# Loads and layer norm around the mixing stage of an encoder layer: weights moved behind the last output product, first tile's norm spread over four tiles, first tile reordered

## The reference

```python
proj = x @ w_in                                   # 1024 -> 2048: gate b, gate c, value, pool input (512 each)
y_conv = gate_b * short_conv3(gate_c * value)     # depthwise, centred, 3 taps
y_pool = (window_mean(pool_in, 2/4/8/16) - pool_in) @ pool_w * pool_scale   # per group of 128 channels
x1 = layer_norm(alpha * x + concat(y_conv, y_pool) @ w_out, g1, b1)
y = layer_norm(alpha * x1 + square(relu(x1 @ w_ff1)) @ w_ff2, g2, b2)
```

## Time and profile before

| | |
|---|---|
| median of 6 runs | 1308.21 us (1306.96 to 1308.37) |
| profiled execution, time | 1307.83 us |
| profiled execution, span of its slowest core (core 5) | 1306.3 us |
| spans of the eight cores | 1296.3 to 1306.3 us |
| TensorE busy in that span | 94% |
| VectorE, ScalarE, GpSimd busy | 48%, 18%, 11% |

### The profile page before, as it was taken

One profiled execution on the slowest core, in us unless ns is written; L12 is line 12 of the kernel. 1 busy time (PEld: TensorE's weight loads), 2 busy tenths in 40 slices (PEclk: granted clock), 3 DMA queues, 4 the chain that ended last, 5 costly groups with the idle time before them and its releaser, 6 DMA issues.

```text
span 1306.3 us, 16633 instructions; the slowest of 8 cores (1296.3 to 1306.3 us)
## 1 busy us (share of the span) xinstructions
PE 1233.2 (94%) x5760; PEld 565.1 (43%) x5760; DVE 620.7 (48%) x948; ACT 239.9 (18%) x497; POOL 140.6 (11%) x158
## 2 busy tenths in 40 slices
PE   4899979999955999999999999999999999999996
PEld 3544434444422444444444444444444444444442
DVE  1457446444501813853581482376348148435324
ACT  2322112222200310320230031023013003202300
POOL 4335234321400000000000000000000000000000
PEclk9999998999987999999999999999999999999998
DMA  9963775975599442361242245226124423702001
GB/s 135 187 127 84 172 145 170 219 148 177 128 197 241 142 130 97 107 184 65 97 144 83 97 137 154 97 89 187 31 110 136 127 97 113 178 33 98 1 1 65
DMA packets 75106, 160.90 MB, mean 123 GB/s; under 512 B 38544, under 2 KB 38544, under 8 KB 71824
## 3 DMA queue, kind: packets, MB, share of 16 engines
q1 hardware_dynamic: 63984, 119.59, 27.4%
q0 software_dynamic: 11040, 40.24, 19.2%
HBM read 126.66 MB, written 56.62 MB: 140 GB/s over the span
## 4 chain that ended last, share of the span: by engine, by line
PE 87%; DMA 9%; DVE 1%; issue 1%; POOL 1%; ACT 0%; DVEq 0%; ACTq 0%; SPq 0%; POOLq 0%
PE bank L281 87%; DMA ring<-xe 6%; DMA scr_xb<-ring 1%; DMA scr_z<-ring 1%; DMA win<-w_in 1%; DVE ring L288 1%; POOL H L292 0%; DVE H L292 0%; DVE H L288 0%; ACT H L285 0%; PE bank L358 0%; ACT L285 0%; ACT win L285 0%; DVE st L462 0%; DVE wff L288 0%
## 5 line engine op out<-in xcount | busy, mean ns | idle before, releaser
L281 PE MATMUL bank<-xT,wff 128*128 128x512 bf16 x2048 | 447.7, 381 | 30.8 <-DVE ring L288 30.8
L281 PEld LDWEIGHTS bank<-xT,wff 128*128 128x128 bf16 x2048 | 201.1, 98 | 276.2 <-issue 37.6
L288 DVE SCALAR_TENSOR_TENSOR ring<-ring,bank 128x512 f32<-128x512 f32 x128 | 81.5, 684 | 462.2 <-PE bank L281 381.7
L285 ACT ACTIVATE H<-bank 128x512 f32<-128x512 f32 (+1 forms) x292 | 169.2, 591 | 368.3 <-PE bank L281 267.0
L281 PE MATMUL bank<-win,H 128*128 128x512 bf16 x1024 | 224.1, 379 | 0.0
L292 DVE TENSOR_TENSOR H<-H 128x512 bf16<-128x512 f32 x256 | 173.2, 687 | 82.4 <-ACT H L285 82.1
L281 PE MATMUL bank<-wout,H 128*128 128x512 bf16 x768 | 171.4, 382 | 4.4 <-DVE wff L292 4.4
L281 PEld LDWEIGHTS bank<-win,H 128*128 128x128 bf16 x1024 | 100.2, 98 | 120.8
L281 PE MATMUL bank<-xT,win 128*128 128x512 bf16 (+1 forms) x608 | 118.8, 356 | 24.7 <-DMA win<-w_in 16.7
L292 POOL TENSOR_TENSOR H<-H 128x527 f32<-128x527 f32 (+2 forms) x80 | 100.8, 1260 | 226.0 <-ACT H L285 188.0
L281 PEld LDWEIGHTS bank<-wout,H 128*128 128x128 bf16 x768 | 75.6, 98 | 96.5 <-issue 7.1
(11 more groups left out here) (35 smaller groups left out, 347.5 us busy)
## 6 DMA issues: line engine op xcount, KB each, us to landing
ring<-xe SPq DMA_DIRECT2D x32, 512.0 KB, 15.4
scr_x<-ring SPq DMA_DIRECT2D x32, 512.0 KB, 2.8
ring<-scr_x SPq DMA_DIRECT2D x32, 512.0 KB, 9.7
y<-ring SPq DMA_DIRECT2D x32, 512.0 KB, 2.9
scr_z<-ring SPq DMA_DIRECT2D x28, 512.0 KB, 14.0
ring<-scr_z SPq DMA_DIRECT2D x28, 512.0 KB, 5.7
wff<-w_ff POOLq DMA_DIRECT2D x8, 1024.0 KB, 19.9
scr_xb<-ring POOLq DMA_DIRECT2D x32, 256.0 KB, 4.0
```

What stands on the lines that cost most here:

```text
L281: pe.emit(lambda h: h.matmul(bank[bi][:, 0:cols], lhsT=lhsT, rhs=rhs, start=start, stop=stop), reads=reads, writes=[B_bank[bi]], signal=si ...
L285: act.emit(lambda h: h.activation(out=out, in_=in_, func=func, **kw), reads=reads, writes=writes, excl=excl)
L288: dve.emit(lambda h: h.scalar_tensor_tensor(out=out, in0=in0, scalar=scalar, in1=in1, op0=op0, op1=op1), reads=reads, writes=writes, excl= ...
```

## The change

The four blocks of `w_ff2` that were loaded after `proj(7)` now stand behind `w_ff1` block 7, after `wo(7)`; two of the x loads of tile 7 go ahead of `wo(6)`. Tile 0's z is stored to `scr_z` like any other; block i of it is loaded back at the first hook of `proj(i + 2)`, i = 0 to 3, and its pieces are popped one at each hook; x of the next tile is always loaded at the second hook. In tile 0, x is loaded as two halves of four channel blocks behind the first `w_in` block, `pw` comes in a layout with 2 KB runs and later, the order of blocks follows the new order of `proj(0)`: value, gate c, gate b, pool, with the pool part one group later and the gate product straight behind its matmuls. The diff, cut to its core:

```diff
-    pw_d = din("pw", [4, 128, 128])
+    pw_d = din("pw", [128, 4, 128])
...
-        load_xT(0)
         load_win(0)
-        load(pool, pwb, pw_d.rearrange("g c d -> c g d"), S_pw, [], [B_pw])
-        for j in range(4):
-            if j:
+        for hh in range(2):
+            load(pool, xT0[:, 4 * hh:4 * hh + 4, :], xet[0][:, 4 * hh:4 * hh + 4, :], S_x0[hh], [], [B_x0[hh]])
+        load_win(4)
+        load_win(8)
+        load_win(1)
+        load(pool, pwb, pw_d, S_pw, [], [B_pw])
+        for j in range(1, 4):
+            if j > 1:
                 load_win(j)
-            load_wpt(3 - j)
+            load_wpt(4 - j)
             load_win(4 + j)
+            if j == 3:
+                load_wpt(0)
             load_win(8 + j)
         load_xT(1)
...
+            def gates(j):
+                u = j % 2
+                (bi, _, _), = chunk(i, 8 + j)
+                gate.append(lambda: a_tt(dve, ycat[:, j, :], bank[bi][:], acc[u], ALU.mult, [B_acc[u]],
+                                         [By[j]], excl=[B_bank[bi]]))
+
+            if i == 0:
+                for j in range(4):
+                    conv(j, [4 - j] if j else [], [0] if j == 3 else [])
+                    gates(j)
+                    gate.pop()()
+                    if j:
+                        late.append(mix(4 - j))
+                late.append(mix(0))
+                return
+            for j in range(4):
+                conv(j)
+                pooled = mix(3 - j)
+                gates(j)
                 late.append(pooled)
...
-                    if not keep:
-                        load(sp, scr_z[i, s], ring[r][:], S_rs[r], B_ring[r], [B_scz[i][s]])
+                    load(sp, scr_z[i, s], ring[r][:], S_rs[r], B_ring[r], [B_scz[i][s]])
...
-            wo(i, i + 1, ld, keep=i == 0)
-            if i < 2:
-                for s in (0, 1) if i == 0 else (2, 3):
-                    pieces += ln1_pieces(0, s, xr_slot[(0, s)], s)
-            hk = [lambda: pop(3)] * 4
-            hk[2 if i < 2 else 1] = lambda i=i: (pop(3), xr_hook(i + 1)())
+            wo(i, i + 1, ld)
+
+            def ln_hook(i=i):
+                pop(1)
+                if i < NS:
+                    load_z(0, i)
+                    pieces.extend(ln1_pieces(0, i, z_slot[(0, i)], i))
+
+            def xr(i=i):
+                pop(1)
+                for s in range(NS):
+                    load_xr(i + 1, s)
+
+            hk = [ln_hook, xr, lambda: pop(1), lambda: pop(1)]
...
-        alias_barrier(B_wff2[1:5], B_win)
-        for g in range(1, 5):
-            load_wff2(g)
+        for s in range(2):
+            load_xr(NT - 1, s)
         wo(NT - 2, NT - 1)
-        for s in range(NS):
+        for s in range(2, NS):
             load_xr(NT - 1, s)
         wo(NT - 1)
...
         alias_barrier(B_wff2[6:8], [B_wout])
+        alias_barrier(B_wff2[1:5], B_win)
         load_wff1(7)
-        for g in range(5, 8):
+        for g in range(1, 8):
             load_wff2(g)
```

More of the change, by code:

```diff
@@ L233, in build_program @@
         B_xT = [Buf("xT0"), Buf("xT1")]
+        B_x0 = [Buf("x00"), Buf("x01")]
         B_win = [Buf(f"win{c}") for c in range(16)]
@@ L262, in build_program @@
         S_xT = [dsem("d_xT0"), dsem("d_xT1")]
+        S_x0 = [dsem("d_x00"), dsem("d_x01")]
         S_win = [dsem(f"d_win{c}") for c in range(12)]
@@ L371, in chunk @@
                         mm(b[q], HALF, win[:, c, k, :], xT[0][:, k, HALF * q:HALF * q + HALF], k == 0, k == 7,
-                           [B_win[c], B_xT[0]], k == 7)
+                           [B_win[c], B_x0[k // 4]], k == 7)
                 return [(b[0], HALF, 0), (b[1], HALF, HALF)]
@@ L377, in chunk @@
                 mm(b[0], 512, win[:, c, k, :], xT[i % 2][:, k, c0:c0 + 512], k == 0, k == 7,
-                   [B_win[c], B_xT[i % 2]], k == 7)
+                   [B_win[c], B_x0[k // 4] if i == 0 else B_xT[i % 2]], k == 7)
             return [(b[0], 512, c0)]
@@ L398, in proj, with conv @@
             gate = []
-            for j in range(4):
-                g = 3 - j
+            def conv(j, w_after_v=(), w_after_c=()):
                 u = j % 2
@@ L403, in proj @@
                     a_act(vS[u][:, c0:c0 + w], bank[bi][:, 0:w], AF.Copy, [], [B_vS[u]], excl=[B_bank[bi]])
-                if i == 0:
+                for g in w_after_v:
                     wprime(g)
@@ L408, in proj @@
                          [B_vS[u]], [B_gcv[j]], excl=[B_bank[bi]])
+                for g in w_after_c:
+                    wprime(g)
                 if gate:
@@ L417, in proj, with mix @@
                     late.pop(0)()
+            def mix(g):
                 for bi, w, c0 in chunk(i, 12 + g):
@@ L431, in proj @@
                     step += 1
-                (bi, _, _), = chunk(i, 8 + j)
-                gate.append(lambda j=j, bi=bi, u=u: a_tt(dve, ycat[:, j, :], bank[bi][:], acc[u], ALU.mult, [B_acc[u]],
-                                                         [By[j]], excl=[B_bank[bi]]))
                 def pooled(g=g, wd=wd, cur=cur, cur_b=cur_b):
@@ L446, in pooled @@
                              [B_tmp8, B_pS[g]], [By[4 + g]])
+                return pooled
+            def gates(j):
[16 more added lines that the diff above has]
+                gates(j)
                 late.append(pooled)
@@ L486, in build_program, with wo @@
         korder = [0, 7, 1, 6, 2, 5, 4, 3]
-        def wo(i, carry_tile=None, loads=(), keep=False):
+        def wo(i, carry_tile=None, loads=()):
             q = i % 2
@@ L516, in gb_load @@
                          S_gb, writes=[B_gb])
-        def xr_hook(i):
-            def h():
-                for s in range(NS):
-                    load_xr(i, s)
-            return h
-        nop = lambda: None
         proj(0)
         late_flush(0)
+        alias_barrier([B_xT[0]], B_x0)
         load_xT(2)
@@ L529, in build_program @@
         gb_load(g1_d, b1_d)
-        proj(1, [nop, xr_hook(0)])
+        proj(1, [lambda: None, lambda: [load_xr(0, s) for s in range(NS)]])
         alias_barrier([B_wff1[5]], [B_pw])
@@ L691 @@
     cw = np.ascontiguousarray(f(conv_w)[0].reshape(3, 4, 128).transpose(2, 1, 0).reshape(128, 12))
-    pw = f(pool_w)[0]
+    pw = np.ascontiguousarray(f(pool_w)[0].transpose(1, 0, 2))
     psc = np.ascontiguousarray(f(pool_scale)[0].reshape(4, 128).T)
```

## The result

The changed kernel takes 1263.11 us (median of 10 runs, 1262.6 to 1263.28), 0.9657 of the kernel before (95% interval 0.9648 to 0.9665): 45 us less, where 41.6 were forecast. Executions in which the cores of one die showed a lower granted clock than the others are left out of all times and ratios in this text.

A forecast was written before the change was run, and what follows sets the result against it. The prediction took TensorE's work plus its waits and slow matmuls as the bound. First tile -3.8, layer norm -16.5 and seam -21.3 sum to -41.6 us, from 1308.2 to 1266.6 us, range 1250 to 1285.

The forecast's parts named there:

- What bounds: Whole kernel: TensorE, busy 94% of the span; only its waits and its stretches at lower clock can be won.
- First tile: Start to the second tile's projection: earlier first loads and no 1.5 us waits, -3.8 us, bounds 0 and -8.
- Layer norm of the first tile: Mixing tiles: z through DRAM, one block per tile, removes waits and slow matmuls, -16.5 us, bounds -16.5 and 0.
- Rival (b): Mixing tiles: late z or x loads lose as much as the old way, the 16.5 us stay; 1283.1 us, chance 0.12.
- The seam: Last output product to MLP: 35.3 us of loss goes, 14 us of new loss behind late z comes, -21.3 us.
- Rival (a): Seam to the MLP: z loads come in time, so the 14 us fall away; 1252.6 us, chance 0.18.
- Rival (c): Seam: q1 starves until the weights' flood is over, 41.4 us lost in place of 14; 1294 us, chance 0.08.
- Rival (d): Four mixing tiles: x loads land 37 us after issue, four tiles lose 57 us, slower than before; 1324 us, chance 0.03.
- The sum: Whole kernel: -3.8 - 16.5 - 21.3 = -41.6 us from a median of 1308.2, forecast 1266.6 us, chance 0.56.

The follow-up runs named there:

- a part alone: Kernel before with only the first tile's changes (x in two halves, order of loads, gate product behind its matmuls): 0.995, 6.5 us less.
- the one-line kernel: Kernel before with one edit, in the first tile the gate product straight behind its own matmuls: 0.9945, 7 us less.
- the kernel with the late pieces: Changed kernel with the second tile's layer norm pieces begun at step 13 of the first MLP region instead of step 2: 1249.25 us.
- the earlier z: Changed kernel with the first two z loads of the second tile ahead of the last output product: 1251.11 us.

## Why the prediction was right, point by point

- **What bounds.** TensorE plus its waits: the gain is the waits and the slow matmuls behind them, and nothing else moved. From the second MLP product to the end both kernels take the same (1306.3 - 466.49 = 839.8 us, 1261.8 - 422.22 = 839.6).
- **First tile**, -3.8 forecast, -5.9 between the two slowest cores (-6.4 in the mean of the eight, 54.9 to 48.5), -6.5 as a part alone. Right in its place, in its arrival times (TensorE starts at 12.92 and goes on at 16.27 and 26.29, for 13.0, 16.4 and 25.8) and in its next wait (0.38 us for the second tile's x, which I had put 3 us off), too small in size. The term that was mis-sized is the sum of what is left after chunk 9: I took 0.138 us for a matmul of 264 columns by dividing a row of 39, but 8 of those are gate matmuls of 512 columns. In the profile after, 56 of them take 33.43 - 26.29 = 7.14 us; less 8 of 0.2158, 48 take 5.41, which is 0.113 each. Then 128 take 14.4 us in place of 17.6, and 51.7 becomes 48.5; the eight cores have 47.1 to 49.6 (on the slowest, chunk 9 begins about 0.6 us later than forecast, and the wait for x adds 0.38). That the gate product's place takes the three waits away is shown by the one-line kernel; the halves of x that I priced into the bound are shown to be worth nothing, because the stops and slow matmuls behind an early start use it up.
- **Layer norm of the first tile**, -16.5 forecast, -16.5 found on core 5's stretch (306.59 to 290.07). Rival (b) is excluded: TensorE has no wait in a mixing tile, and VectorE stands 6.6 us in all for z there, which TensorE's banks cover, as worked out.
- **The seam**, -35.3 + 14 = -21.3 forecast, 104.4 - 82.6 = -21.8 found. z was expected 27.6 us after the end of the last output product (403.5 - 375.9); it came after 26.2 (379.64 - 353.46). The long wait was 9.6 us for 10.9 forecast, behind 88 matmuls as worked out. That the sum came so close is in part luck: of the 82.6 us, 13.5 are lost (without a wait the stretch takes 69.1, as in the kernel with the late pieces), for 14 forecast, but the waits make 10.7 of them for 13.5, and slow matmuls 2.8 for 0.5. Behind the long wait 64 matmuls take 16.32 us, 0.255 each, with a granted clock of 0.84 between 382 and 398, a mean over the levels 1.2 and 2.4 GHz; with the late pieces it was 1.00 there, 2.4 GHz throughout. Rival (a) gave 1252.6 us for a z in time; it takes a further edit to get there, 1251 us with the earlier z (1249 with the late pieces, where z is as late as ever). Rival (c), starvation, is excluded by 704 packets against 700. Rival (d) is excluded by the seven tiles without a wait.
- **The sum.** -41.6 forecast, -45 measured (-44.5 between the two profiled spans). The rest is the first tile's term (2 to 3 us) and half a microsecond at the seam.
- **What I expected of the experiments** fared worse: that the seam's gain hung on x and not on the weights' place. That step was not in the prediction's sum, and the run with the weights in their old place refuted it.

By "DMA: Bandwidth & Descriptors" of the Trainium skill, Anatomy of one DMA, a transfer issued by GpSimd takes 2.0 us and its bytes at 436 GB/s; carried over to SP's queue, an estimate, that would have had z there in 5.6 us. The trace does not agree for a queue beside the weights: z came after 26.2 us, and the z load in the chain of waits of the changed kernel, the third block's, took 37.41 us:

```profile
358.69 37.41 DMA ring<-scr_z
```

## What to carry to other kernels

Price a wait by the engine that stands in order behind it, not by the transfer alone: at the seam the same late z cost 10.7 us of waits and 2.8 of slow matmuls, or nothing, depending on where its first reader was put in VectorE's list. Before splitting or moving loads, follow the stage to its end: in the first tile here an early first half gained nothing, because TensorE stood for the second half and for what came behind it. And when a queue of large weight packets starts, count what is already waiting on the small one: every 512 KB still there put off all that followed by about 8 us here.

## What the runs showed that I had not expected

A load may come early and still not help, because the slot that it needs hangs on a store in the same traffic (20 us for a store of 512 KB, then 33.6 us for the load). And a delay of 3.6 us in four stores (from 5.9 to 2.3 us ahead of the region) became one of 7.6 us in the load behind them. My reading is that it moved about one store from the quiet side of the weights' start to the busy side; what the trace shows is that the last two stores landed 6 us later (18.5 for 12.5).
